# Moving tiles placed two 64-byte steps from the weights, and the last swiglu's tiles aligned, in a fused fp32 two-block transformer kernel

## The reference, cut to what matters

```python
def swiglu(h, w_gate, w_up, w_down):
    return (jax.nn.silu(h @ w_gate) * (h @ w_up)) @ w_down
# first_block: layer 0 = pool mixer, layer 1 = stick-breaking attention (q, k, v of 16 heads)
    for i in range(DEPTH):
        a = rmsnorm(h, norm_mix[i])
        ...
        h = h + mix
        h = h + swiglu(rmsnorm(h, norm_ffn[i]), ffn_w_gate[i], ffn_w_up[i], ffn_w_down[i])
# second_block: neighbourhood attention and a hyena mixer, gated, then its own swiglu
        x = x + g1 * gated_merge(gna, ghy, y_na, y_hy, w_na_o[i], w_hy_o[i], w_out[i])
        h2 = modulate(rmsnorm_2(x, norm2_g[i]), sh2, sc2)
        x = x + g2 * swiglu_2(h2, ffn_w1[i], ffn_w3[i], ffn_w2[i])
```

## Time and profile before

| | |
|---|---|
| median of 3 runs | 1011.05 us (1009.72, 1011.05, 1015.68) |
| the profiled execution | 1009.55 us, span 1007.5 us |
| TensorE busy | 970.8 us, 96% of the span, 7884 matmuls |
| VectorE busy | 821.9 us, 82% |
| ScalarE busy | 563.0 us, 56% |
| granted TensorE clock | 0.998 of full speed |
| HBM | 189 GB/s over the span |

### The profile page before, as it was taken

How to read it: one execution, slowest core, us unless ns; L and a number is a source line. 1 busy time by engine, 2 the same in 40 slices (tenths; PEclk the granted TensorE clock), 3 DMA queues, 4 the chain that set the end, 5 groups by cost and what they waited for, 6 DMA issues and landing times.

```text
span 1007.5 us, 19368 instructions
## 1 busy us (share of the span) xinstructions
PE 970.8 (96%) x7884; PEld 947.9 (94%) x7884; DVE 821.9 (82%) x1386; ACT 563.0 (56%) x1054; POOL 111.5 (11%) x134
## 2 busy tenths in 40 slices
PE   7999999999999999999999999899999999999996
PEld 6999999999899989999999998899999999999996
DVE  7989898887999967999979867998997668766543
ACT  6745455345777646555554536666554466555532
POOL 4100000211000004002203301231002100000000
PEclk9999999999999999999999999999999999999999
DMA  9555657765442315988867813433446336554441
GB/s 281 224 192 206 215 203 258 247 232 209 148 139 104 136 63 199 341 321 294 285 228 284 317 47 111 173 109 114 147 139 223 141 130 229 201 194 168 168 168 42
DMA packets 33880, 192.17 MB, mean 191 GB/s; under 512 B 4976, under 2 KB 6272, under 8 KB 15104
## 3 DMA queue, kind: packets, MB, share of 16 engines
q1 hardware_dynamic: 23440, 157.36, 43.3%
q10 hardware_dynamic: 6912, 25.17, 7.4%
q0 software_dynamic: 3440, 8.42, 2.7%
HBM read 187.78 MB, written 3.15 MB: 189 GB/s over the span
## 4 chain that ended last, share of the span: by engine, by line
PE 67%; DVE 19%; ACT 8%; issue 3%; DMA 2%; POOL 0%; SPq 0%; DVEq 0%; ACTq 0%
PE ps L93 66%; DVE wl L70 6%; ACT wh L67 3%; DMA raw<-w 2%; PE ps L96 1%; DVE a L70 1%; DVE b L70 1%; ACT u L67 1%; DMA cst<-cst 1%; DVE s L77 1%; DVE c L81 1%; DVE l L73 1%; ACT s L67 1%; DVE natl L70 0%; ACT a L67 0%
## 5 line engine op out<-in xcount | busy, mean ns | idle before, releaser
L70 DVE TENSOR_TENSOR wl<-raw,wh 128x1024 fp32r<-128x1024 f32 x283 | 343.1, 1227 | 23.3 <-ACT wh L67 22.8
L67 ACT ACTIVATE wh<-raw 128x1024 fp32r<-128x1024 f32 x286 | 296.0, 1049 | 28.9 <-PE ps L93 12.3
L93 PE MATMUL ps<-xh,wh 128*128 128x256 f32 (+1 forms) x992 | 278.4, 281 | 3.2 <-DVE wl L70 2.0
L93 PE MATMUL ps<-xl,wh 128*128 128x256 f32 x992 | 276.6, 279 | 0.0
L93 PE MATMUL ps<-xh,wl 128*128 128x256 f32 (+1 forms) x992 | 276.6, 279 | 0.0
L93 PE MATMUL ps<-xt,wh 128*128 128x272 f32 (+1 forms) x1120 | 218.0, 290 | 2.2 <-DVE fg L70 1.0
L93 PEld LDWEIGHTS ps<-xh,wh 128*128 128x128 f32 x992 | 186.6, 188 | 4.1 <-issue 2.4
L93 PEld LDWEIGHTS ps<-xh,wl 128*128 128x128 f32 x992 | 187.1, 189 | 0.2
L93 PEld LDWEIGHTS ps<-xl,wh 128*128 128x128 f32 x992 | 186.9, 188 | 0.0
L93 PEld LDWEIGHTS ps<-xt,wh 128*128 128x128 f32 x1120 | 177.3, 188 | 3.9 <-DVE fg L70 1.5
L93 PE MATMUL ps<-xt,wl 128*128 128x272 f32 (+1 forms) x560 | 159.9, 286 | 0.0
(11 more groups left out here) (348 smaller groups left out, 1586.8 us busy)
## 6 DMA issues: line engine op xcount, KB each, us to landing
raw<-w SPq DMA_DIRECT2D x141, 1024.0 KB, 4.9
ada<-ada ACTq DMA_DIRECT2D x42, 512.0 KB, 4.5
cb<-ada ACTq DMA_DIRECT2D x6, 512.0 KB, 4.1
raw<-w SPq DMA_DIRECT2D x4, 512.0 KB, 6.6
spare<-w SPq DMA_DIRECT2D x2, 1024.0 KB, 9.3
spectra<-ev POOLq DMA_DIRECT2D x8, 256.0 KB, 3.8
skew<-rpb POOLq DMA_DIRECT2D x8, 192.0 KB, 3.6
x<-x POOLq DMA_DIRECT2D x2, 544.0 KB, 9.4
```

The lines of the kernel that those rows point to most:

```text
L67: return Issued(self.e and self.e.activation(out, src, func, **kw))
L70: return Issued(self.e and self.e.tensor_tensor(out, a, b, op))
L93: return Issued(self.e and self.e.matmul(out, stat, mov, start=start, stop=stop))
```

## The change

All moving operands go to place 0, and the place of the operands under `UNDER` goes along, so that they stay one step below, in terms of `line`, from 0 to 6. `XT`'s low part starts 320 numbers after the high one, at place 0 too. The last swiglu gets views of its own: `XW` with a stride of 320 numbers (1280 bytes), so that each of the eight high tiles starts at place 0, and `XV` for the low part behind it. `ZS` starts one step lower to reach place 0. No instruction is added, removed or moved: on each of the five engines the rows of both programs are the same in kind, shape and order (7273 rows on TensorE, 1318 on VectorE), but for the addresses.

```diff
-LINES, STILL, MOVING, UNDER = 8, 2, 1, 0
+LINES, STILL, MOVING, UNDER = 8, 2, 0, 6
...
-PAIR = 640
+PAIR, LOW, WIDE = 640, 320, 320
...
+        self.XW = self.at("xw", self.x0, DT * WIDE, F32R)
+        self.XV = self.at("xv", self.x0 + 4 * DT * WIDE, DT * TR, F32R)
...
-        return self.XT[:, PAIR * d:PAIR * d + T1] if n == T1 else self.XH[:, n * d:n * d + TR]
+        return self.XT[:, PAIR * d:PAIR * d + T1] if n == T1 else self.layout(n)[0][:, n * d:n * d + TR]
 
     def xl(self, d, n):
-        return self.XT[:, PAIR * d + 352:PAIR * d + 352 + T1] if n == T1 else self.XL[:, TR * d:TR * d + TR]
+        return self.XT[:, PAIR * d + LOW:PAIR * d + LOW + T1] if n == T1 else self.layout(n)[1][:, TR * d:TR * d + TR]
+
+    def layout(self, n):
+        return (self.XW, self.XV) if n == WIDE else (self.XH, self.XL)
 
     def xs(self, n, t0=0, w=None):
-        if n == 258:
-            return [self.XH[:, n * d:n * d + n] for d in range(DT)], [self.xl(d, n) for d in range(DT)]
+        if n == WIDE:
+            return [self.XW[:, n * d:n * d + 258] for d in range(DT)], [self.xl(d, n) for d in range(DT)]
...
-        z = self.line(self.off["nqh0"] - 64, MOVING)
+        z = self.line(self.off["nqh0"] - 128, MOVING)
...
-            self.norm_hi(A, "mod", d, M0, TR, self.small[:, 16 + d:17 + d], 258)
+            self.norm_hi(A, "mod", d, M0, TR, self.small[:, 16 + d:17 + d], WIDE)
...
-        return self.XH[:, :8 * 258].rearrange("p (d c) -> p d c", d=8)[:, :, 256:258]
+        return self.XW[:, :].rearrange("p (d c) -> p d c", d=8)[:, :, 256:258]
...
-            self.norm_lo(V, "mod", d, M0, TR, self.small[:, 16 + d:17 + d], 258)
+            self.norm_lo(V, "mod", d, M0, TR, self.small[:, 16 + d:17 + d], WIDE)
...
-        xh, xl = self.xs(258)
+        xh, xl = self.xs(WIDE)
```

## The result

The changed kernel takes 1024.12 us (median of four runs, 1023.81 to 1024.74) where the kernel before took 1010.82 (1009.72 to 1015.68): a ratio of 1.0124 with an interval of 1.0101 to 1.0148. It is slower by about 13 us. The forecast was 1000.0 us in a range of 994 to 1009, so it had the wrong sign.

The account below looks back on a forecast made before the run. The prediction took TensorE to bound the kernel, sharing parts of the chain with VectorE. Its terms, 3.1 + 5.0 + 0.9 + 0.3 + 0.3 = 9.6 us off 1009.55, gave 999.95, so a median of 1000.0 us, range 994 to 1009.

Parts of the forecast that it names:

- What bounds the kernel: Whole kernel: TensorE, busy 96% of the span, sets the end in pieces of 113, 228, 170 and 22.6 us.
- the rival of ports without contention: All TensorE matmuls: two independent read ports, so place has no part and time stays at 1010.5 us; chance 0.05.
- Suppose each matmul has its own cost by its place: H[0]'s tiles: means of 371.4 to 382 ns a triple solved into one price for each of four places.
- 2*E1 + E3: XT's triple before, priced from places 1 (123.4 ns) and 3 (127.0): 373.8 ns, checked against 373.4 measured.
- Term A: XT, 272 columns, in pool, first swiglu and attention: 10.4 ns less a triple, 3.1 us together.
- Term B: Last swiglu, aligned at place 0: triples from 360.8 to 345 ns, 16 ns less on 316, 5.0 us.
- Term C: 256-column operands from place 1 to 0: fast rhythm unchanged, slow rhythm ended on 71 triples by 13.3 ns, 0.9 us.
- second rival: 256-column triples, second swiglu and last down projection: place 0 settles in the slow rhythm, 10.6 us lost, 1020.5 us; chance 0.08.
- E0: Price of one 272-column matmul at place 0, solved from H[0]'s tiles: 120.3 ns, lowest of the four.
- Terms D and E: CH and XH as stationary operands of 512-column matmuls, 0.3 us; q's views of XT leaving the weights' place, 0.2 us.

Follow-up runs that it names:

- e5: Changed kernel with the weights moved to place 1 and UNDER to 7, moving operands still at place 0, so one step apart: 1007.31 us, one execution.
- e6: Changed kernel with weights at place 3, moving operands at place 1 and UNDER at 7, so two steps apart: 1025.2 us, one execution.
- e2: Changed kernel's layouts kept, but places set back to one step as in the kernel before (MOVING 1, UNDER 0): 1008.25 us, ratio 0.9963 to the kernel before.
- e10: e2 with the last swiglu's operands alone moved to three steps from the weights: 1008.46 us, one execution.
- e3: Changed kernel with moving operands three steps from the weights (MOVING 7, UNDER 4): 1015.11 us, one execution.
- e9: e2 with the context's norm sum matmul issued before feature 20 of the second swiglu instead of behind down block 0: 1009.75 us, ratio 0.9975 to the kernel before.
- e12: The same program as e10, timed over six executions: 1006.91 us, ratio 0.9963 to the kernel before.
- e4: Changed kernel with moving operands at the weights' own place, no step between (MOVING 2, UNDER 2): 1025.34 us, one execution.

## Why the prediction was wrong

**What bounds the kernel** was read rightly: the pieces of the chain that grew are the ones that it named as TensorE's own, and the two pieces of the first swiglu lost 1.1 us, where the 171 triples of `XT` that the prediction put in them make 1.0 at 5.8 ns each.

**That distances depend on addresses** was right, and the rival of ports without contention (0.05) failed: same instructions, same order, 13 us apart. The Trainium skill's sentence on two independent read ports (TensorE: Matmul & The Clock Gate, "Step-by-step: what each phase is for") speaks of bandwidth and not of addresses. Read as the prediction read it, that placement is free, it doesn't hold here: e5 and e6, 340 and 360 ns in the second swiglu, show that the two operands' addresses act on each other. The runs don't show by what part of the chip.

**The step that failed** is this one: "Suppose each matmul has its own cost by its place". It made four prices from a stretch in which the place changed with every tile, and put the best of them (120.3 ns at place 0) on every matmul. Measured with the place held: 126.6 ns (379.9 for three). Two equations for two unknowns can't fail, and the one check, on `XT` before, tested nothing of the kind: 2*E1 + E3 is the very equation from which E1 and E3 were solved (the hidden tiles with high 1, low 3, 373.9 ns), so it compared only two operands at the same places. And the trace of the kernel before spoke against prices by place. From 130 to 155 us `XT`'s triples, all at the same places (1, 1, 3), take 381, 373, 368 and 371 ns in turn (worked out from the trace's start times): at one set of places they spread as far as the 371 to 382 that the prediction put down to place. That a rhythm of TensorE carries over from one matmul to the next stood in the earlier trace rows already, where equal places had two speeds. A cost per place can't give that, and I took it as a detail instead of as a refutation.

**Term A** (`XT`, a gain of 10.4 ns a triple): a loss of 5.8. With one step and the new offset of the low part it is a gain of 3.7 (e2), so the layout was worth something and the distance took it away.

**Term B** (last swiglu, a gain of 16 ns): a gain of 0.9, from 360.8 to 359.9. Aligned at one step it gains 4.1, and aligned at three 6.1 (e2, e10), where 16 was forecast.

**Term C** ("In the fast rhythm nothing is above the floor, so nothing is won", and the slow rhythm ended by "a wider berth") carries the loss. The 340 ns of the second swiglu were themselves an effect of one step, not a floor that any place reaches. The second swiglu's piece alone lost 9.5 us, and the last swiglu's piece 2.5, in which the down projection lost 2.8 (176 triples by 15.8 ns) and the up projection won 0.3. The prediction's second rival (0.08) had this place, size and sign: 800 triples by 13.3 ns, 1020.5 us; measured, 16 to 18 ns and 1024.1. Its mechanism was near but not the same: what came wasn't the slow rhythm of 353, but rhythms of 356 to 360 that the kernel before doesn't have at 256 columns in these stages. Its argument against itself, that E0 is the lowest price, was the failed step again.

**Terms D and E** are too small to be told apart in the end time. q's views did come from 352.6 to 349.8 ns, and to 340.8 in e6, both at one step.

What stays open: why whole odd steps allow 340 ns; why 272 columns never came to the 360 that the prediction works out for them; whether the good distances repeat every 128, 256 or 512 bytes (e3's mixed result speaks against a plain 128, and the times of the hidden tiles, which stand 17 steps apart and repeat every four tiles, 371, 374, 382 and 379 ns, speak for 256); and what exactly of an interruption chooses the rhythm. Other distances than the six shown (0, 32, 64, 96, 128 and 192 bytes) were not tried at 256 columns; all count from the moving operand's place up to the weights'.

## What to carry to other kernels

In a stream of matmuls that each load new weights, the distance of moving and stationary operand in SBUF, in 64-byte steps, can be worth 5% of TensorE's pace; try the distances on the chip for each width of moving operand that matters, and keep the layout that was measured with the place held. Don't take the price of a steady state from a stretch in which the quantity changes at every step, and when a trace has the same instructions at two speeds, treat a price per instruction as refuted until a run says otherwise.

## What the runs showed of the hardware that was not expected

- TensorE holds a rhythm. At one step, 256-column triples run at 340 or 353 ns until a matmul of another kind or a wait comes between them, which can change the rhythm or leave it, and the interruption's place in the program sets where the change falls (e9). Even the same program shows both in the same stretch of two executions (e10, e12). That could explain why the kernel before spreads from 1009 to 1016 us and the changed one, which has no 340 ns to lose, only from 1023.8 to 1024.7; this is argued, not shown.
- At a fixed distance a rhythm can have a period: 378 and 382 ns by turns (`XT` after), 381, 373, 368, 371 (`XT` before), 354, 355, 359, 351, 361 (256 columns after), or one value, 360 (e4).
- Moving both operands by one 64-byte step leaves every class as it was within 0.4 ns (e2 and e5), but for what the rhythm after an interruption adds. It isn't so at two steps: from the changed kernel to e6 the second swiglu goes from 356 to 360 ns.
- Half steps do no good: 355 ns at 32 bytes and 356 at 96 in the second swiglu, where 64 bytes give 340; whether by the distance or by the start off a 64-byte step, no run tells.
